# First modulation of a two-layer backbone kernel: eight passes over the inputs, or two groups of outputs

## The reference

```python
mx = (jax.nn.silu(c) @ w_mod[l] + b_mod[l]).reshape(B, N_MOD, 1, D)      # 9 vectors of 1024
mc = (jax.nn.silu(c_ctx) @ w_mod[l] + b_mod[l]).reshape(1, N_MOD, 1, D)
x = x + 0.5 * mx[:, 2] * swiglu(modulate(rms_norm(x), mx[:, 0], mx[:, 1]), ...)
# modulate(h, shift, scale) = h * (1 + scale) + shift
```

## Time and profile before

| | us |
|---|---|
| Median of 3 runs | 2782.57 (2780.73 to 2783.06) |
| Profiled execution, its own time | 2780.36 |
| Its span | 2778.6 |
| PE busy | 2686.4 (97%) |
| DVE busy | 2032.6 (73%) |
| ACT busy | 1248.3 (45%) |
| POOL busy | 263.1 (9%) |
| PE's first product of the opening | starts at 42.13 |
| PE's first product of tile 2 | starts at 63.17 |

### The profile page before, as it was taken

How to read it: one execution, slowest core, us unless ns; L and a number is a source line. 1 busy time by engine, 2 the same in 40 slices (tenths; PEclk the granted TensorE clock), 3 DMA queues, 4 the chain that set the end, 5 groups by cost and what they waited for, 6 DMA issues and landing times.

```text
span 2778.6 us, 42501 instructions
## 1 busy us (share of the span) xinstructions
PE 2686.4 (97%) x16327; PEld 2559.6 (92%) x16327; DVE 2032.6 (73%) x3501; ACT 1248.3 (45%) x2254; POOL 263.1 (9%) x279
## 2 busy tenths in 40 slices
PE   7999999999988899999999999999999998999999
PEld 5999999989978789999999999999988987889998
DVE  6888878854477758887878578787875587677875
ACT  4242424343488742424243434343443488544543
POOL 1000000040333210000000100000012234000000
PEclk9999999999999999999999999999999999999999
DMA  6334342322100224343433223324223102233233
GB/s 234 120 99 145 99 141 95 122 71 68 33 14 10 78 77 128 100 135 109 129 107 114 88 80 107 114 91 137 92 83 89 46 14 56 82 102 105 91 107 91
DMA packets 288341, 264.09 MB, mean 95 GB/s; under 512 B 11982, under 2 KB 266356, under 8 KB 287120
## 3 DMA queue, kind: packets, MB, share of 16 engines
q1 hardware_dynamic: 286608, 256.86, 30.3%
q10 hardware_dynamic: 896, 4.46, 0.4%
q0 software_dynamic: 640, 0.09, 0.0%
HBM read 255.08 MB, written 2.10 MB: 93 GB/s over the span
## 4 chain that ended last, share of the span: by engine, by line
PE 84%; DVE 7%; ACT 5%; issue 2%; POOL 0%; DMA 0%; SPq 0%; DVEq 0%; POOLq 0%; ACTq 0%
PE pair L487 12%; PE pair L488 12%; PE pair L495 12%; PE pair L1159 9%; PE pair L1161 9%; PE pair L1160 9%; PE pmid L2622 2%; PE pair L1819 2%; PE pair L1821 2%; PE pair L1820 2%; PE psum L1161 1%; PE psum L1159 1%; PE psum L1160 1%; PE pair L750 1%; PE pair L751 1%
## 5 line engine op out<-in xcount | busy, mean ns | idle before, releaser
L487 PE MATMUL pair<-s_six,d_tile 128*128 128x384 f32 (+1 forms) x1160 | 398.1, 343 | 0.5 <-DVE s_six L1660 0.5
L488 PE MATMUL pair<-s_six,d_tile 128*128 128x384 f32 (+1 forms) x1160 | 397.3, 343 | 0.0
L1043 DVE SCALAR_TENSOR_TENSOR pmid<-mod_raw,cs_rows 128x1024 f32<-128x1024 f32 x256 | 314.0, 1227 | 4.4
L1327 ACT ACTIVATE p_hi<-p_raw 128x512 fp32r<-128x512 f32 x360 | 224.7, 627 | 205.1 <-DVE p_raw L1357 115.4
L1628 DVE SCALAR_TENSOR_TENSOR xT<-pair,mv,xT 128x384 f32<-128x384 f32 (+2 forms) x320 | 149.4, 515 | 208.1 <-PE pair L495 203.9
L1159 PE MATMUL pair<-h_lo,p_hi 128*128 128x384 f32 (+1 forms) x864 | 278.4, 322 | 5.7 <-ACT sg L1372 5.7
L1159 PE MATMUL pair<-t_lo,p_hi 128*128 128x384 f32 (+1 forms) x864 | 277.8, 321 | 0.6 <-ACT sg L1372 0.6
L1160 PE MATMUL pair<-h_hi,p_hi 128*128 128x384 f32 (+1 forms) x864 | 277.6, 321 | 0.0
L1161 PE MATMUL pair<-h_hi,p_lo 128*128 128x384 f32 (+1 forms) x864 | 277.6, 321 | 0.0
L1160 PE MATMUL pair<-t_hi,p_hi 128*128 128x384 f32 (+1 forms) x864 | 277.6, 321 | 0.0
L1161 PE MATMUL pair<-t_hi,p_lo 128*128 128x384 f32 (+1 forms) x864 | 277.5, 321 | 0.0
(11 more groups left out here) (368 smaller groups left out, 6451.5 us busy)
## 6 DMA issues: line engine op xcount, KB each, us to landing
mod_raw<-in_w_mod_rows SPq DMA_DIRECT2D x128, 512.0 KB, 3.3
p_raw<-in_w_ffn_gate SPq DMA_DIRECT2D x36, 1024.0 KB, 5.6
p_raw<-in_w_ffn_up SPq DMA_DIRECT2D x36, 1024.0 KB, 5.5
d_raw<-in_w_ffn_down SPq DMA_DIRECT2D x96, 384.0 KB, 3.5
w_raw<-in_w_in SPq DMA_DIRECT2D x32, 512.0 KB, 4.0
w_raw<-in_w_ffn_gate SPq DMA_DIRECT2D x16, 512.0 KB, 3.9
w_raw<-in_w_ffn_up SPq DMA_DIRECT2D x16, 512.0 KB, 4.1
d_raw<-in_w_ffn_down SPq DMA_DIRECT2D x32, 256.0 KB, 2.8
```

The costliest lines, as they stand in the source:

```text
L487: eng.matmul(dst, wh, rl, start=k == 0, stop=False)
L488: eng.matmul(dst, wh, rh, start=False, stop=False)
L1043: eng.scalar_tensor_tensor(pmid[:, 0:D_MODEL], mod_raw[:, m % 2, :], 1.0, cs_rows[:, j, :], ALU.mult, ALU.mult, accum_out=mod[:, m, j:j + ...
L1327: eng.activation(chunked(p_hi[n]), src, ACT.Copy).then_inc(g_hi, 1)
```

## The change

The first modulation is computed in two groups of outputs instead of eight passes over the input chunks. Group g holds half of the shift columns and half of the scale columns (1024 outputs), for all eight input chunks, with rows of 2 KB. All of `mod_first` is now issued by SP: group 0 after the rows of `x`, group 1 after the first two weight tiles. `mod_product(g)` has 16 matmuls; the stripe in `pmid` is now chosen by input chunk (k % 4), and the four stripes are added in `mod_turn`, which multiplies `mod_rows` as weights with a column of ones and zeros (`row_sum`) into `psum2`. The chunks 0 to 3 of `h` follow group 0 and the chunks 4 to 7 group 1. `x_unit` is gone: the first norm uses the scheme of the later ones, with POOL for the odd chunks. PE multiplies both parts of a chunk at once, in both first tiles, and does the product and the turn of group 1 between chunks. Both spreads of the conditions stand at the end of the opening.

```diff
-MOD_GROUP = 4
+MOD_GROUP = 8
+MOD_GROUPS = START_MOD // MOD_GROUP
+GROUP_CHUNKS = KD // MOD_GROUPS
...
         def first_spread(eng):
             eng.wait_ge(n_rstd, 2)
-            eng.wait_ge(acc_free[0], N_START // 2)
-            rows = pair[0][:, 0:SEQ].rearrange("p (g r c) -> p r g c", g=COL_GROUPS, r=ROWS)
+            rows = psum2[:, 0:SEQ].rearrange("p (g r c) -> p r g c", g=COL_GROUPS, r=ROWS)
...
-        def first_unit_rows(eng, k):
...
+        def first_open_pe(eng, tiles):
+            for k in range(KD + 1):
+                if k % GROUP_CHUNKS == 2 and k // GROUP_CHUNKS + 1 < MOD_GROUPS:
+                    mod_product(eng, k // GROUP_CHUNKS + 1)
+                if k % GROUP_CHUNKS == 3 and k // GROUP_CHUNKS + 1 < MOD_GROUPS:
+                    mod_turn(eng, k // GROUP_CHUNKS + 1)
+                if k == KD - 1:
+                    cs_spread_out(eng, 0)
+                for j, (t, o) in ((1, tiles[1]), (0, tiles[0])):
+                    c = k - j
+                    if not 0 <= c < KD:
+                        continue
+                    if c == 0:
+                        eng.wait_ge(w_lo_done, t.n(1))
+                        eng.wait_ge(acc_free[o.odd], o.half())
+                    if j == 0:
+                        wait_low(eng, 2 * (c + 1))
+                    for p, (a, b, _) in enumerate(norm_parts(0)):
+                        part_product(eng, o, c, wtile(t), h_moving, a, b, c == 0, c == KD - 1, acc_done if p else None)
+            cs_spread_out(eng, 1)
+
+        def first_open_act(eng):
+            for k in range(KD):
+                for p in range(2):
+                    norm_hi(eng, 0, p, k)
+                if k % GROUP_CHUNKS == 2 and k // GROUP_CHUNKS + 1 < MOD_GROUPS:
+                    mod_row_copy(eng, k // GROUP_CHUNKS + 1)
+            cs_rows_copy(eng, 0)
+            split_hi(eng, Nth(2, 1, 0), WIDTHS[2], Nth(0, 1, FF_O0[0]))
+            cs_rows_copy(eng, 1)
+
+        def first_open_dve(eng):
+            for k in range(0, KD, 2):
+                if k % GROUP_CHUNKS == 0:
+                    first_vectors(eng, k // GROUP_CHUNKS)
+                for p in range(2):
+                    norm_scale(eng, 0, p, k)
+                if k == 0:
+                    split_lo(eng, Nth(0, 1, 0), WIDTHS[0])
+                for p in range(2):
+                    norm_scale(eng, 0, p, k + 1)
+                for p in range(2):
+                    norm_lo(eng, 0, p, k)
+                if k == 0:
+                    split_lo(eng, Nth(1, 1, 0), WIDTHS[1])
...
+        def mod_product(eng, g):
+            eng.wait_ge(mod_first_loaded[g], 32)
+            if g:
+                eng.wait_ge(mod_row_copied, g)
+            for k in range(KD):
+                at = k % MOD_STRIPES * MOD_STRIPE
+                for a in range(0, MOD_GROUP * P, 512):
+                    last = eng.matmul(pmid[at:at + 2, a:a + 512], cs[:, k, :], mod_first[:, g, k, a:a + 512],
+                                      start=k < MOD_STRIPES, stop=k >= KD - MOD_STRIPES)
+            last.then_inc(mod_done, 1)
+
+        def mod_row_copy(eng, g):
+            eng.wait_ge(mod_done, g + 1)
+            if g:
+                eng.wait_ge(mod_turned, g)
+            eng.activation(mod_rows[:, :], pmid[:, 0:MOD_GROUP * P], ACT.Copy).then_inc(mod_row_copied, 1)
+
+        def mod_turn(eng, g):
+            eng.wait_ge(mod_row_copied, g + 1)
+            eng.wait_ge(row_sum_step, MOD_STRIPES - 1)
             for u in range(MOD_GROUP):
-                last = eng.transpose(pmid[:, u * P:(u + 1) * P], mod_rows[:, u * P:(u + 1) * P], ident[:, :])
+                at = TURN_AT_COL + 2 * (MOD_GROUP * g + u)
+                last = eng.matmul(psum2[:, at:at + 2], mod_rows[:, u * P:(u + 1) * P], row_sum[:, :], start=True, stop=True)
             last.then_inc(mod_turned, 1)
+
+        def first_vectors(eng, g):
+            eng.wait_ge(mod_turned, g + 1)
+            for which, group, add in ((0, 1, 1.0), (1, 0, 0.0)):
+                n = GROUP_CHUNKS
+                at = TURN_AT_COL + 2 * (MOD_GROUP * g + n * group)
+                bias = vecs[:, 0, V_BMOD + group * KD + n * g:V_BMOD + group * KD + n * (g + 1)]
+                eng.scalar_tensor_tensor(mv[:, which, n * g:n * (g + 1), :],
+                                         psum2[:, at:at + 2 * n].rearrange("p (t j) -> p t j", j=2),
+                                         add, bias.rearrange("p (t a) -> p t a", a=1).broadcast_to([P, n, 2]), ALU.add, ALU.add)\
+                   .then_inc(mv_ready, 1)
...
-        def first_mod_load(eng, k):
-            eng.dma_start(mod_first[:, k, :], w_mod[0][k * P:(k + 1) * P, 0:START_MOD * P]).then_inc(mod_first_loaded[k], 16)
+        def first_mod_load(eng, g):
+            w = MOD_GROUP * P // 2
+            for group in range(2):
+                src = w_mod[0].rearrange("(k p) n -> p k n", p=P)[:, :, group * KD * P + g * w:group * KD * P + (g + 1) * w]
+                eng.dma_start(mod_first[:, g, :, group * w:(group + 1) * w], src).then_inc(mod_first_loaded[g], 16)
...
         def _(sp):
-            for k in range(KD // 2, KD):
-                first_mod_load(sp, k)
+            first_mod_load(sp, 0)
             first_loads(sp, blocks[0])
+            for g in range(1, MOD_GROUPS):
+                first_mod_load(sp, g)
...
         def _(pe):
-                if o >= 2:
-                    mod_product(pe, o - 2)
...
             first_spread(pe)
-            for k in range(KD // 2, KD):
-                mod_product(pe, k)
-            mod_turn(pe)
+            mod_product(pe, 0)
+            mod_turn(pe, 0)
...
         def _(act):
-            for k in range(KD // 2):
-                first_mod_load(act, k)
...
-                        open_act(act, X_NORM[0, 0])
+                        first_open_act(act)
```

More of the change, by code:

```diff
@@ L543, in chunks_at, with chunk_no @@
             return 2 * KD * q
+        def chunk_no(q, p, k):
+            return chunks_at(q) + (KD * p + k if q else 2 * k + p)
         def on_pool(i):
             q, p, k = i // (2 * KD), i // KD % 2, i % KD
-            return norms[q]["tail"] and k % 2 == 1 and not (norms[q]["late"] and p == 1)
+            if q == 0:
+                return i // 2 % 2 == 1
+            return k % 2 == 1 and not (norms[q]["late"] and p == 1)
         def pool_chunks(n):
@@ L789, in open_pe @@
         def open_pe(eng, q, tiles, cols):
[L791 to L794, removed]
+            at = chunks_at(q)
+            lhs = [third_slot, fourth_slot(q)]
             (a, b, _), (a2, b2, _) = norm_parts(q)
@@ L867, in open_act @@
[L867 to L880, removed]
-                norm_rstd(eng, q, 0)
-                tail_residual(eng, q, 2, o6)
+            split_hi(eng, t6 + 4, KD * P, o7 if behind_pairs(q) else o6)
@@ L904, in open_dve @@
                 norm_lo(eng, q, 1, k + 1)
[L905 to L906 removed]
+            split_lo(eng, t6 + 4, KD * P)
         def open_pool(eng, q):
[L910 to L913 removed]
+            for i in range(2 * KD):
+                p, k = (i // KD, i % KD) if q else (i % 2, i // 2)
+                if on_pool(chunk_no(q, p, k)):
+                    norm_lo_pool(eng, q, p, k)
         def rest_act(eng, q, n):
@@ L929, in program @@
         X_NORM = {}
-        mv_count = 0
+        mv_count = 2 * MOD_GROUPS - 4
         for l in range(DEPTH):
@@ L963, in gate_vectors @@
             eng.wait_ge(gate_ready, 2 * (3 * l + b + 1))
-        MOD_STRIPE = P // (START_MOD // MOD_GROUP)
-        def mod_product(eng, k):
-            eng.wait_ge(mod_first_loaded[k], 16)
-            for n in range(START_MOD // MOD_GROUP):
-                last = eng.matmul(pmid[MOD_STRIPE * n:MOD_STRIPE * n + 2, 0:MOD_GROUP * P], cs[:, k, :],
-                                  mod_first[:, k, n * MOD_GROUP * P:(n + 1) * MOD_GROUP * P], start=k == 0, stop=k == KD - 1)
-            if k == KD - 1:
-                last.then_inc(mod_done, 1)
@@ L1168, in ff_pe @@
                     if s == 0 and i == 0:
-                        open_pe(eng, X_NORM[inst // 2, 2 * (inst % 2)], [up_tile(inst, 0, 0, j) for j in range(2)], 2)
+                        tiles = [up_tile(inst, 0, 0, j) for j in range(2)]
+                        if inst:
+                            open_pe(eng, X_NORM[inst // 2, 2 * (inst % 2)], tiles, 2)
+                        else:
+                            first_open_pe(eng, tiles)
                         continue
@@ L2882, in _ @@
                 first_std(act, p)
-            act.wait_ge(mod_done, 1)
-            act.activation(mod_rows[:, :], pmid[:, 0:MOD_GROUP * P], ACT.Copy).then_inc(mod_row_copied, 1)
+            mod_row_copy(act, 0)
             for t in range(2):
@@ L2898, in _ @@
             dve.memset(pmid[:, 0:MOD_GROUP * P], 0.0).then_inc(mod_zeroed, 1)
+            dve.wait_ge(const_loaded, 16)
+            for n in range(1, MOD_STRIPES):
+                first = ident[:, 0:2] if n == 1 else row_sum[:, :]
+                if n > 1:
```

(2 more changed lines are left out.)

122 lines of the change are left out of this document (49 added, 73 removed).

## The result

| | us | ratio to the kernel before, same chip |
|---|---|---|
| before, 4 runs | 2781.93 | |
| changed, 4 runs | 2797.57 (2790.48 to 2798.09) | 1.0049 [1.0036, 1.0061] |
| changed, timed again, 6 runs | 2791.61 (2789.59 to 2792.46) | 1.0035 [1.0022, 1.0047] |
| profiled execution before | 2780.36, span 2778.6 | |
| profiled execution changed | 2790.48, span 2788.6 | |

The change is slower by 0.35 to 0.5%; the forecast was 2788.4 in 2781.5 to 2797.0. The median of the first four runs lies 0.6 us above that range, that of the six further runs inside it. The profiled execution is 10.1 us longer than that of before, where my sum said 5.8. First the chain and the stages, in the columns of the earlier trace rows.

What follows compares the result with a forecast made beforehand. It took PE as the bound, so the start of tile 2 (63.17 us before) sets the total. Its terms put tile 2 at 69.0, +5.8 on the profiled 2780.36, plus 2.2 to the median: 2788.4, range 2781.5 to 2797.

Steps and rivals of the forecast that it cites:

- The sum up to tile 2: Terms from group 0's landing through PE's opening, ending at 64.4, plus 3.4 us idle: 67.8, before the clock charge.
- the charge for the clock: Half clock of PE after the idle time before tile 2: 1.2 us charged, putting tile 2 at 69.0.
- Landing of group 0: Transfer of the first modulation group: landed at 23.4 us (22.9 to 24.9), including 0.5 for rows of 2 KB.
- Product of group 0: 16 matmuls on PE after the landing, four stripes at once: 4.8 us, ending at 28.2.
- Copy and turn: ACT's copy with hand-over 1.1 us, then PE's 8 fp32 matmuls 2.5 us: ending at 31.8.
- First `nt`: DVE's first `nt` after 0.4 us for `mv`: at 32.2, against 39.25 before.
- First product: PE's first product 4.4 us after the first `nt`, behind DVE's scales, split and low parts: 36.6, against 42.13.
- Opening: PE from first product to end: products 19.4 us plus 8.4 for group 1, spreads and waits, 36.6 to 64.4.
- End of the opening: ACT's 5.4 us chain after tile 0, of which PE covers 2.04: idle before tile 2 grows from 0.53 to 3.4.
- Rival A: Modulation products: only two stripes run at once, 3.4 us more for each group; +12.6, 2795.2 us; chance 0.28.
- Rival B: Not slower: front at full clock, idle at the end costs no clock, clock kept into opening; -0.1, 2782.5; chance 0.12.
- Rival C: Group 1's matmuls run beside products on PE, so 3.4 us vanish; +2.4, 2785 us; chance 0.10.

Runs made afterwards that it cites:

- end_closed: Changed kernel with both spreads of the conditions earlier in the opening and the Silu table loaded before the copy of group 0: 2786.82 us, 1.0019 to before.
- before_pause: Kernel before with only the second spread of the conditions moved after tile 1's last products: 2787.25 us, 1.0017 to before.
- skip_group1: Changed kernel without product, copy and turn of group 1; chunks 4 to 7 use group 0's vectors: 2784.47 us, 1.0009 to before.
- one_pass: Kernel before, modulation still in eight passes, with only the change's norm scheme (no `x_unit`, POOL for odd chunks): 2781.16 us, 0.9991 to before.
- one_pass_again: The same kernel as one_pass, timed again: 2780.34 us, 0.9995 to before.
- early_split: Changed kernel with the splits of weight tiles 0 and 1 before group 0's copy on ACT and before the first vectors on DVE: 2788.71 us, 1.0019 to before.
- both: Changed kernel with the changes of end_closed and early_split together: 2786.62 us, 1.0014 to before.
- one_pass_dve1: one_pass with the low part of the first odd chunk on DVE instead of POOL: 2782.54 us, 1.0000 to before.

## Why the prediction came out as it did

The way of the change was as forecast: an earlier first `nt`, part of it given back before the first product, and the rest and more in the opening and at its end. The sum up to tile 2, without the charge for the clock, was 67.8; it was 67.54. That the two are so near is in part luck: the first product came 1.15 later than the sum had it (37.75 against 36.6), and the opening was 1.3 shorter.

- **Landing of group 0:** 23.4 forecast. Its product started at 24.80, within the stated bounds of 22.9 to 24.9. PE had waited 3.45 us for it.
- **Product of group 0:** 4.8, measured 4.90, the first part at half clock. Copy and turn: forecast end 31.8, measured 32.84. First `nt`: 32.2, measured 33.22; the landing is 1.4 late, and the turn at full clock took 1.95 instead of 2.5.
- **First product:** 4.4 behind `nt`, measured 4.53.
- **Opening:** 27.8 from the first product to the end of PE's work, measured 26.5. The 1.4 are 0.37 of waits instead of 0.9, and a shorter stretch of half clock: it ends at 41.0, 3.3 us behind the first product, where I had taken over the 5.4 of before.
- **End of the opening:** 3.4 idle before tile 2, measured 3.33, by the very chain that I had added up. end_closed and before_pause show it from both sides.
- **Rival A** (stripes don't overlap) is wrong. Weight loads start in fours, 0.43 us apart at full clock (0.85 in the half-clock part of group 0), and 32 records take 3.63 us at full clock. The rival's price was 6.8. The strict order of matmuls that the Trainium skill states (TensorE: Matmul & The Clock Gate, section The mechanism) had spoken for it; these 3.63 us don't agree with it.
- **Rival B** (front at full clock, end covered) is wrong: 0.68 in 13 to 24.8 us, and 3.33 us idle before tile 2.
- **Rival C** (group 1 beside products) is wrong: no product lies among the 32 records from 42.58, and skip_group1 gives back 6.2 us.

The term that was mis-sized is the clock. I charged 1.2 us behind the idle time and nothing further on. Measured against before, the changed kernel lost up to 1.8 us between tile 2 and the norm at 560 us, where its stretch from 68.4 lies, and another 3.9 us from there to the end. The sum fell short of the profiled execution by 4.3 us, and these two less the 1.2 are 4.5, with tile 2 itself 0.3 early.

The later stretches I can't lay at the change's door one by one. They stand in places that the change doesn't touch, as the one in the earlier trace rows does, and some come and go between executions: one_pass and one_pass_again are the same kernel and had 22.3 and 10.2 us. But the one near 566 us is not mere chance. It is there in all six executions in which tile 2 started at 64.4 or later (changed, changed again, end_closed, early_split, before_pause, both) and in none of the other six, and it made the piece between the first two `psum<-ones,acc` of the table 11.1 to 12.3 us long instead of 10.5. before_pause has it without any change to the modulation, so it isn't tied to the groups. That it goes with the late start is what these twelve show; why is open. Whether the changed kernel gets more of the others by its nature stays open too.

Its first set lay at 2797.57 and its second at 2791.61; the account above covers the second. What added about 7 us to three of the first four runs was not profiled. Their granted clocks were 0.987, 0.988 and 0.990, where the profiled one had 0.992 and the second set 0.991 to 0.993, so they had more half clock, and in which places is open.

## What to carry to other kernels

Work that is taken out of the shadow of a transfer and put in line on the engine that sets the end costs its full time: here 6.0 us against 4.4 won at the first product. Before moving a last small step (here eight transposes of 1.0 us) behind the products, follow the other engine's chain that hangs on it to its end (copy, table load, Silu): here 2.8 us idle, and the clock after it. And when only a part of such a change is of use, try it alone: the norm scheme without the groups put tile 2 1.5 us ahead of before instead of 4.4 behind, though the times can't tell that gain from none.

## What the runs showed of the hardware

**A split on DVE and a low part on POOL shut one another out.** In one_pass POOL's low part started at 39.53 and took 1.40 us; DVE's split started at 39.72 and took 2.30 instead of 1.22, that is, until 1.09 us after POOL had ended. In one_pass_again it was 2.29, and in one_pass_dve1, with nothing on POOL beside it, 1.22. In the changed kernel DVE's split of tile 1 started first (37.52, 1.22 us) and POOL was the one that waited: its first record took 2.28 us (the three durations are the shortest, the median and the longest of its eight low parts):

```profile
L731 POOL TENSOR_TENSOR h_lo<-nt,h_hi x8: 730/1006/2282, 37.6 to 58.2; 128x512 fp32r<-128x512 f32 x4, 128x256 fp32r<-128x256 f32 x4
```

The other three records of that size took 1.27 to 1.30. The Trainium skill, SBUF — State Buffer, section SBUF: two separate sides, says that a DVE operation with two inputs from SBUF and a GpSimd operation that reads SBUF exclude one another for a whole instruction, and that the first to start keeps the port. The traces agree in both directions. A scale that reads `xT` and `psum2` kept its 0.74 us beside POOL (44.80 in one_pass); the low part at 45.66, with both inputs in SBUF, took 0.95 where others took 0.74 to 0.77.

**An idle time of 3.3 us before tile 2 was followed by half clock in each of the five profiled executions that had it** (changed, changed again, early_split, before_pause, skip_group1), and idle times of 0.53 or 0.90 us in none of the seven others. The stretch began 0.2 to 1.4 us behind the start of tile 2, in before_pause 1.0 before it. Nothing between 0.90 and 3.33 us was tried, and the length of the idle time alone doesn't decide: elsewhere 1.49 us were followed by half clock and 2.69 us were not the earlier trace rows.

**A microsecond at 1.2 GHz cost less than half a microsecond** in most places. Right behind tile 2 the 3.4 us cost up to 1.8, but the other prices are about 1.8 us for the 6.8 at 566.7, 2.0 for the 10.2 of before at 890.6 and 921.4, and 0.3 for each over the twelve executions.

**Rows of 2 KB** moved at 379 to 391 GB/s as group 0 came in (single microseconds from 18 to 23) and at 373 to 395 with group 1 (28 to 37), mostly nearer to the 418 of 8 KB than to the 350 of 1 KB. Three of group 1:

```profile
28.00:29.00 1.00, 1.00 (x12) 0.23 (x8) 0.00 (x0) 0.00 (x0) 0.00 (x0) 1.00 1.10 395
32.00:33.00 1.00, 0.83 (x8) 0.74 (x7) 0.13 (x2) 0.72 (x1) 0.00 (x0) 1.00 1.05 387
36.00:37.00 1.00, 0.00 (x0) 0.00 (x0) 1.00 (x3) 0.81 (x2) 0.00 (x0) 0.50 1.03 381
```
